# A two-block fp32 transformer layer: a weight piece and the inputs taken in halves, one mLSTM head scored earlier, two steps moved to POOL and ACT

## What is computed

```python
k, v = split(rmsnorm(mem, g_mem) @ w_mem_kv)             # memory keys and values
q_a, k_a, ... = split(rmsnorm(x, g_mix) @ w_in)
u = rms_norm(x, norm_g) @ w_in                            # mLSTM and pool layer
xm, om, gates, zm, xp, zp = split(u)
xc = silu(causal_conv(xm, conv_w, conv_b))                # width 4
q, k = xc_h @ w_q, xc_h @ w_k * 256 ** -0.5               # per head of 256
v = xm_h @ w_v
hm = mlstm(q, k, v, gates) * sigmoid(om)
hm = rms_norm per head, + skip * xc, * silu(zm)
out = concat(hm, pool(xp) ...) @ w_out + x
```

## Time and profile before

| | |
|---|---|
| median of 3 runs | 819.34 us (818.83 to 819.68) |
| the profiled execution | 819.23 us |
| its span | 817.4 us |
| PE, DVE, ACT, POOL busy | 794.1, 568.0, 432.3, 131.0 us |
| mean granted clock of TensorE | 0.992 |
| DMA | 142.78 MB, 175 GB/s in the mean |

### The profile page before, as it was taken

The page is one execution under the profiler, slowest core; times in us unless marked ns, Lnnn a source line. Parts: engine busy times, 40 slices in busy tenths (PEclk is TensorE's granted clock), DMA queues, the critical chain, the costliest instruction groups (busy, mean ns, idle before and its releaser), DMA issues.

```text
span 817.4 us, 11950 instructions
## 1 busy us (share of the span) xinstructions
PE 794.1 (97%) x4616; PEld 693.7 (85%) x4616; DVE 568.0 (69%) x946; ACT 432.3 (53%) x585; POOL 131.0 (16%) x99
## 2 busy tenths in 40 slices
PE   8799999999999999999999999999999979999998
PEld 7688788888888899999988888989799868877776
DVE  5645556796468678787864485769865795997774
ACT  5834544344544466566553374555736343788450
POOL 0002740000000004544431000041005000024000
PEclk9899999999999999999999999999999999999999
DMA  9977433334455465554555545435565414634211
GB/s 342 360 278 247 155 139 123 145 109 163 152 202 192 168 245 210 165 197 176 186 172 191 203 148 170 170 134 155 191 214 200 154 52 155 251 127 154 87 52 52
DMA packets 23364, 142.78 MB, mean 175 GB/s; under 512 B 3564, under 2 KB 4472, under 8 KB 7312
## 3 DMA queue, kind: packets, MB, share of 16 engines
q1 hardware_dynamic: 20160, 134.51, 46.0%
q0 software_dynamic: 1376, 3.43, 1.4%
q10 hardware_dynamic: 1776, 4.12, 1.4%
HBM read 140.97 MB, written 2.64 MB: 176 GB/s over the span
## 4 chain that ended last, share of the span: by engine, by line
PE 78%; DVE 13%; ACT 4%; issue 2%; DMA 2%; SPq 0%; ACTq 0%; DVEq 0%
PE gemm L488 16%; PE gemm L490 15%; PE gemm L489 15%; PE gemm L494 8%; PE gemm L495 8%; PE gemm L496 8%; DVE wlo L1662 4%; ACT whi L1161 2%; DMA raw<-in_weights 2%; DVE xc L2183 2%; PE head L554 1%; PE head L885 1%; PE head L744 1%; PE head L884 1%; PE head L905 1%
## 5 line engine op out<-in xcount | busy, mean ns | idle before, releaser
L1662 DVE TENSOR_TENSOR wlo<-raw,whi 128x2048 fp32r<-128x2048 f32 x122 | 282.1, 2314 | 115.9 <-ACT whi L1161 115.7
L1161 ACT CAST whi<-raw 128x2048 fp32r<-128x2048 f32 x122 | 232.6, 1906 | 210.1 <-PE gemm L490 124.3
L488 PE MATMUL gemm<-whi,x0hi 128*128 128x512 f32 (+2 forms) x400 | 158.0, 395 | 5.7 <-DVE x0lo L1849 4.2
L490 PE MATMUL gemm<-whi,x0lo 128*128 128x512 f32 (+2 forms) x400 | 154.6, 386 | 0.0
L489 PE MATMUL gemm<-wlo,x0hi 128*128 128x512 f32 (+2 forms) x400 | 154.3, 386 | 0.0
L494 PE MATMUL gemm<-x1hi,whi 128*128 128x256 f32 x400 | 113.5, 284 | 0.0
L495 PE MATMUL gemm<-x1lo,whi 128*128 128x256 f32 x400 | 113.2, 283 | 0.0
L496 PE MATMUL gemm<-x1hi,wlo 128*128 128x256 f32 x400 | 113.2, 283 | 0.0
L488 PEld LDWEIGHTS gemm<-whi,x0hi 128*128 128x128 f32 x400 | 75.7, 189 | 22.1 <-DVE x0lo L1849 4.9
L490 PEld LDWEIGHTS gemm<-whi,x0lo 128*128 128x128 f32 x400 | 75.5, 189 | 15.0
L489 PEld LDWEIGHTS gemm<-wlo,x0hi 128*128 128x128 f32 x400 | 75.8, 190 | 13.5
(11 more groups left out here) (344 smaller groups left out, 1346.6 us busy)
## 6 DMA issues: line engine op xcount, KB each, us to landing
raw<-in_weights SPq DMA_DIRECT2D x122, 1024.0 KB, 4.8
raw<-in_weights SPq DMA_DIRECT2D x4, 512.0 KB, 6.3
bias_rows<-bias_row POOLq DMA_DIRECT2D x1, 1536.0 KB, 15.6
memt<-in_memt SPq DMA_DIRECT2D x4, 256.0 KB, 5.3
tok<-in_mem SPq DMA_DIRECT2D x1, 1024.0 KB, 7.7
xt<-in_xt SPq DMA_DIRECT2D x2, 512.0 KB, 11.1
xres<-in_x ACTq DMA_DIRECT2D x1, 1024.0 KB, 6.5
bias<-bias_rows POOLq DMA_DIRECT2D x8, 128.0 KB, 2.9
```

What stands on the lines that cost most here:

```text
L488: mm(o, xh, wh, start=start, stop=False)
L490: return mm(o, xl, wh, start=False, stop=stop)
L1161: nc.scalar.copy(whi[:, p % RING, :], raw[:, p % RING, :]).then_inc(s_hi, 1)
L1662: V.tensor_tensor(wlo[:, p % RING, :], raw[:, p % RING, :], whi[:, p % RING, :].bitcast(F32), ALU.subtract).then_inc(s_lo, 1)
```

## The change

- Piece 2 is split in halves and multiplied by `first_pieces`, at its own bank. The load of the larger part of the parameters goes behind that of the memory, and the half scalings that need it to step 4.
- The squares of the memory are summed in step 0. The input pairs are scaled two in step 1 and two in step 2, and PE waits for two pairs before piece 4 and for all before piece 5.
- The first two xm pieces wait for chunk c - 4.
- `x1hi` and `x1lo` of xc are taken without the factor 0.5, which goes into the emptying of wq and wk; the low parts are taken by POOL.
- `ML0` is 98. Head 0 is scored in wk after its third chunk, and everything of the heads comes one step earlier.
- `rsqrt` has two steps of a higher order, nine operations in all instead of eleven.
- DVE multiplies the root by half and by the reciprocal, and ACT scales the head by it.

```diff
-ML0 = p0("aout")
+ML0 = p0("aout") - 1
-SCALED = {"mem": 1, "mix": 3, "ckv": p0("cu") + 3, "cq": p0("ukv")}
+SCALED = {"mem": 0, "mix": 3, "ckv": p0("cu") + 3, "cq": p0("ukv")}
...
             half_piece(1, 1)
-            sp.dma_start(par[:, GAINS:NPAR], ins["params"][:, GAINS:NPAR]).then_inc(s_par, 16)
...
             sp.dma_start(tok[:, 12:14, :, :].rearrange("p a b c -> p (a b c)"), ins["mem"]).then_inc(s_mem, 16)
+            sp.dma_start(par[:, GAINS:NPAR], ins["params"][:, GAINS:NPAR]).then_inc(s_par, 16)
             next_piece(3)
...
                 e = p - ML0
-                if not 0 <= e <= ML_H + 1:
+                if not 1 <= e <= ML_H + 1:
                     return
-                if e == 0:
-                    pe.wait_ge(s_vones, 1)
-                    pe.wait_ge(s_gcol, 1)
-                    pe.wait_ge(s_mixlo, 4)
...
-                for p in range(2):
+                for p in range(3):
+                    o = [bank(p // 2, t) for t in range(T)]
                     for half in range(2):
-                        pair = 2 * p + half
+                        pair = (2 * p + half) % 4
...
-            for p in range(2, Z0):
+            for p in range(3, Z0):
...
-                if p == p0("qkv"):
-                    pe.wait_ge(s_inlo, 8)
+                if p in (p0("qkv"), p0("qkv") + 1):
+                    pe.wait_ge(s_inlo, 6 + 2 * (p - p0("qkv")))
...
-                    chunk_free(pe, c - 2)
+                    chunk_free(pe, c - (4 if name == "xm" and i_ < 2 else 2))
...
+                        if name == "wk" and g == 2:
+                            pe.wait_ge(s_vones, 1)
+                            pe.wait_ge(s_gcol, 1)
+                            ml_score(0).then_inc(s_mo, 1)
...
+                if 1 <= e <= ML_H:
+                    h = e - 1
+                    act.wait_ge(s_mr, h + 1)
+                    for t in range(T):
+                        i = nc.scalar.activation(hm[h % 2][:, t, :], hm[h % 2][:, t, :], ACT.Copy,
+                                                 scale=rstd[:, 16 + 2 * h + t:17 + 2 * h + t])
+                    i.then_inc(s_mn, 1)
...
-                    nc.scalar.activation(x1hi[:, 2 * i:2 * i + 2, :], xc[:, 2 * i:2 * i + 2, :],
-                                         ACT.Copy, scale=0.5).then_inc(s_fhi, 1)
+                    nc.scalar.copy(x1hi[:, 2 * i:2 * i + 2, :], xc[:, 2 * i:2 * i + 2, :]).then_inc(s_fhi, 1)
...
-                                                    ACT.Copy, scale=1.0 if name == "wq" else 1.0 / 16)
+                                                    ACT.Copy, scale=0.5 if name == "wq" else 0.5 / 16)
...
+            split_half(2, 0)
+            split_half(2, 1)
             for p in range(Z0):
-                if p not in LATE_SPLIT:
+                if p not in LATE_SPLIT and p > 0:
                     split(p + 2)
...
-                if p == 2:
-                    input_hi("mix", range(4))
+                if p in (1, 2):
+                    input_hi("mix", (2 * p - 2, 2 * p - 1))
...
-                for n in range(3):
-                    order(V.tensor_tensor(u, dst, dst, ALU.mult))
-                    order(V.tensor_tensor(u, u, v, ALU.mult))
-                    last = V.scalar_tensor_tensor(dst, u, 1.5, dst, ALU.add, ALU.mult)
-                    if n < 2:
-                        order(last)
-                return last
+                order(V.tensor_tensor(u, dst, dst, ALU.mult))
+                order(V.tensor_tensor(u, u, v, ALU.mult))
+                order(V.scalar_tensor_tensor(u, u, 5.0 / 3, u, ALU.add, ALU.mult))
+                order(V.scalar_tensor_tensor(dst, u, 1.25, dst, ALU.add, ALU.mult))
+                order(V.tensor_tensor(u, dst, dst, ALU.mult))
+                order(V.scalar_tensor_tensor(u, u, 3.375, v, ALU.mult, ALU.mult))
+                return V.scalar_tensor_tensor(dst, u, 2.25, dst, ALU.add, ALU.mult)
...
-                    order(V.tensor_tensor(r, r, rsum[:, :], ALU.mult))
-                    for t in range(T):
-                        i = V.tensor_scalar(hm[h % 2][:, t, :], hm[h % 2][:, t, :],
-                                            rstd[:, 16 + 2 * h + t:17 + 2 * h + t], 0.5, ALU.mult, ALU.mult)
-                    i.then_inc(s_mn, 1)
+                    V.scalar_tensor_tensor(r, r, 0.5, rsum[:, :], ALU.mult, ALU.mult).then_inc(s_mr, 1)
...
-                i = p - p0("xm") - 3
-                if 0 <= i < 4:
-                    k = slice(2 * i, 2 * i + 2)
-                    dve.wait_ge(s_fhi, i + 1)
-                    V.scalar_tensor_tensor(x1lo[:, k, :], xc[:, k, :], 0.5, x1hi[:, k, :].bitcast(F32),
-                                           ALU.mult, ALU.subtract).then_inc(s_xclo, 1)
...
+            for g in range(4):
+                pool.wait_ge(s_fhi, g + 1)
+                k = slice(2 * g, 2 * g + 2)
+                Q.tensor_tensor(x1lo[:, k, :], xc[:, k, :], x1hi[:, k, :].bitcast(F32),
+                                ALU.subtract).then_inc(s_xclo, 1)
```

More of the change, by code:

```diff
@@ L324, in program @@
         s_vones = sem("value_ones_ready")
+        s_mr = sem("ml_root_ready")
         s_md = sem("max_rows_moved")
@@ L815, in ml_step @@
                 e = p - ML0
-                if not 0 <= e <= ML_H + 1:
+                if not 1 <= e <= ML_H + 1:
                     return
-                if e == 0:
-                    pe.wait_ge(s_vones, 1)
-                    pe.wait_ge(s_gcol, 1)
-                    pe.wait_ge(s_mixlo, 4)
[L822 to L826, removed]
+                pe.wait_ge(s_mp, min(e, ML_H))
+                if e >= 2:
+                    pe.wait_ge(s_mden, e - 1)
                 if 1 <= e <= ML_H:
@@ L986, in first_pieces @@
             def first_pieces():
-                for p in range(2):
+                for p in range(3):
+                    o = [bank(p // 2, t) for t in range(T)]
                     for half in range(2):
-                        pair = 2 * p + half
+                        pair = (2 * p + half) % 4
                         pe.wait_ge(s_hi if half else s_hi0, p + 1)
                         pe.wait_ge(s_inhi, pair + 1)
[L993 to L996, removed]
+                        order_ = [(t, 2 * pair + j, slice((2 * half + j) * 512, (2 * half + j) * 512 + 512))
+                                  for t in range(T) for j in range(2)]
+                        for t, kb, ws in order_:
+                            mm(o[t][:, :], x1hi[:, kb, t * P:t * P + P], whi[:, p, ws], start=kb == 0, stop=False)
                         pe.wait_ge(s_lo if half else s_lo0, p + 1)
-                        for t, j in order_:
-                            kb, ws, ts = 4 * p + j, slice(j * 512, j * 512 + 512), slice(t * P, t * P + P)
-                            mm(bank(0, t)[:, :], x1hi[:, kb, ts], wlo[:, p, ws], start=False, stop=False)
+                        for t, kb, ws in order_:
+                            mm(o[t][:, :], x1hi[:, kb, t * P:t * P + P], wlo[:, p, ws], start=False, stop=False)
                         pe.wait_ge(s_inlo, pair + 1)
-                        for t, j in order_:
-                            kb, ws, ts = 4 * p + j, slice(j * 512, j * 512 + 512), slice(t * P, t * P + P)
-                            i = mm(bank(0, t)[:, :], x1lo[:, kb, ts], whi[:, p, ws], start=False,
+                        for t, kb, ws in order_:
+                            i = mm(o[t][:, :], x1lo[:, kb, t * P:t * P + P], whi[:, p, ws], start=False,
                                    stop=kb == KB - 1)
@@ L1269, in split_half @@
             def split_half(p, h):
-                act.wait_ge(s_piece[p] if h else s_half_piece[p], 16)
+                act.wait_ge(s_piece[p] if h or p == 2 else s_half_piece[p], 16)
                 nc.scalar.copy(whi[:, p, h * D:h * D + D], raw[:, p, h * D:h * D + D])\
@@ L2239, in _ @@
             split_half(1, 1)
-            dve.wait_ge(s_par, 16)
-            for o, (name, w) in ((0, ("gn", 4)), (4, ("pool_scale", 8)), (12, ("skip", 8))):
-                a = PCOL[name][0]
-                i = V.tensor_scalar(half[:, o:o + w], par[:, a:a + w], 0.5, None, ALU.mult)
-            order(i)
+            split_half(2, 0)
+            split_half(2, 1)
             for p in range(Z0):
@@ L2261, in _ @@
                 gates_dve(p)
-                if p == 2:
-                    input_lo("mix", range(4))
+                if p == 4:
+                    dve.wait_ge(s_par, 16)
+                    for o, (name, w) in ((0, ("gn", 4)), (4, ("pool_scale", 8)), (12, ("skip", 8))):
+                        a = PCOL[name][0]
+                        i = V.tensor_scalar(half[:, o:o + w], par[:, a:a + w], 0.5, None, ALU.mult)
+                    order(i)
+                if p in (1, 2):
+                    input_lo("mix", (2 * p - 2, 2 * p - 1))
                 if p == 20:
```

## The result

The changed kernel took 806.33 us in the median of 4 runs (806.18 to 806.52), the kernel before 819.12 in the same session: a ratio of 0.9843 (95% interval 0.9826 to 0.9860), 12.8 us less. The profiled execution took 806.28 us, with a span of 804.5.

A forecast was written before the change was run, and what follows sets the result against it. PE, busy 97% of the 817.4 us span, was taken as the bound. Gains 6.4 + 1.7 + 3.6 = 11.7, less 1.7 for one new half-speed stretch, net 10.0: 819.2 - 10.0 = 809.2 us, range 803.5 to 814.0.

The forecast's parts named there:

- The start: Before piece 4: PE's 4.15 us wait for the input's low parts and 2.25 of half clock go, 6.4 us saved.
- Piece 2's halves: At the start: splitting piece 2 in halves gains nothing, since PE then idles 1.4 us for piece 3 instead.
- The pool chunk: Before the first xm pieces: PE released 1.6 us earlier and no half clock behind it, 1.7 more, 3.3 us together.
- The lock between DVE and POOL: In xm and om: POOL's low-part operations block DVE for their whole length, 2 x (1.47 - 0.69) = 1.6 us lost.
- The mLSTM heads: Heads one piece earlier: 3.6 us saved, with a loop of 9.3 to 9.4 us a head and some waits left.
- The new half-speed stretch: Behind one of the new idle stretches of 1.9, 1.4 and 2.1 us the clock falls once, 1.7 us lost.
- Elsewhere PE has no gap worth taking: Outside the start, the pool chunk and the mLSTM heads, PE has no idle time worth saving; no gain counted.
- the slower one: Rival, mLSTM heads: ACT's hold delays weight casts, 12.5 us a turn, 822.0 us; decides from 11.8; chance 0.05.
- The lock did not fall the other way: Rival, xm and om: DVE goes first each time and POOL waits, stage worth 4.7 us, 806.2 us; chance 0.09.
- The input halves don't help: Rival, start: later loads make PE wait 3 to 4 us at piece 4 or 6, 813.1 to 815 us; chance 0.10.

The follow-up runs named there:

- the run with all casts first: The changed kernel with ACT's scaling of every mLSTM head moved behind the next weight cast instead of ahead of it: 809.2 us.

## Why the prediction was right

Forecast 809.2, measured 806.33; the range held it. Step by step:

- **The start**, 6.4 forecast, 6.06 measured. The place of the gain was right, and so were the wait that stays at 24 to 25 and the half clock, and PE waits for none of the pieces behind. The credit was not: the text gives the pairs' early place as much part as the squares and does not name the root behind the squares, which held ACT for 2.37 us. By the experiments the squares are worth 4.8, and the remaining 1.2 go to PE's shorter wait or to the early pairs, of which one would have done. The sum came out right without telling these apart.
- **Piece 2's halves**, nothing forecast, nothing measured; the halves were not even what moved the wait.
- **The pool chunk**, 3.3 forecast, 3.07 measured. By the traces 1.57 of it are the wait (2.02 to 0.45) and 1.5 the clock. Undone alone, the wait cost 1.3 at the end of the kernel, and the clock 2.0 in two of four executions and nothing in the others.
- **The lock between DVE and POOL**, two times 1.47 - 0.69 = 1.6 forecast, 1.00 lost in the trace and 1.0 given back by the experiment. The mechanism stands, POOL waiting when DVE turns to the silu; an operation costs DVE 1.10, not 1.47, since POOL, once DVE's subtraction was over, took 1.15 and not 1.47. By the Trainium skill (SBUF — State Buffer, section "SBUF: two separate sides"), an operation that holds the shared port pair keeps it for its whole length and the other blocks; the trace agrees, since DVE's silu lasts 1.78 us and ends when POOL's 2.10 us operation has ended and 0.55 have passed.
- **The mLSTM heads**, 3.6 forecast, 4.07 measured. The loop of 9.3 to 9.4 us a head is 9.27 (636.06 to 645.33). Forecast waits 1.0, 2.1 and 0.5; measured 0.71, 1.86 and 0.55. Undone alone, the earlier start of the heads costs 3.5 and the old root 2.6 (0.7 of it in the attention heads), while ACT's scaling has lost 1.45 against DVE's.
- **The new half-speed stretch**, 1.7 us against the change: this term was wrong. None appeared: the four runs have mean clocks of 0.999 and 1.000 and lie within 0.34 us of each other. The longest wait left, 1.86 (1.85 to 1.88 in the other kernels that have it), did not lower the clock in any profile of these experiments.
- **"Elsewhere PE has no gap worth taking"** was wrong by 0.70 us. The shorter root saves that in the attention heads, where no single wait of PE is above 0.2 us, so that the table of waits does not show it. The old root brings it back.

The forecast's terms as measured give 6.06 + 3.07 - 1.00 + 4.07 = 12.2, and with 0.70 the 12.9 of the spans. Of the 2.9 us by which the forecast was high, 1.7 are the stretch that did not come, 0.7 the root, and the rest the sizes. Of the rivals, the slower one asked for 11.8 us a turn, and the longest in the changed kernel took 9.27. The lock did not fall the other way: POOL went first at all three silus beside it. That this rival's 806.2 is next to the measured time is chance. "The input halves don't help" asked for a wait of 3 to 4 us at piece 4 or 6 because of later loads, and none came; that the early pairs add nothing beside PE's shorter wait has another reason.

## What to carry to other kernels

When a change has several parts at one place, undo each alone: here one number in a table of steps (the squares, moved into a wait for a load) was worth most of the start, while the halves of piece 2, with far more code, were worth nothing. Undoing one part shows what it is worth beside the others: where two parts take away the same wait, each looks worthless alone. Before work goes to an idle engine that shares a port with the busy one, set its price there against what it blocks: 0.69 us saved cost 1.10. Of the two steps that this change moved to POOL and ACT, neither paid: back on DVE they gave 0.96 and 1.45 us. And when an in-order engine must hold for a result, compare for every turn what stands behind it with what that itself waits for; the better order differed between the first head and the last.

## What the runs showed of the hardware

The granted clock's fall from its higher level (2.4 GHz) to half of it behind a wait is not fixed by the length of the wait. The program that waits 2.01 us for a pool chunk ran two executions at a mean clock of 1.000 (807.6) and two at 0.998 (809.7), 2.0 us longer. In the profiles the clock fell after waits of 2.02 (twice), 2.17, 2.18, 2.25, 2.28, 2.45 and 4.15 us, not after others of 2.01 and 2.24, nor after 1.86, and not even after the 3.05 us of the run with all casts first (its stretch of 658 to 668):

```profile
658.00:668.00 10.00, 7.73 (x36) 6.52 (x37) 5.81 (x8) 6.38 (x9) 1.65 (x4) 1.00 0.51 166
```

So a wait of 2 to 3 us has to be priced as itself and a chance of about 2 us more. Kernels with several such waits scattered more: the one with only the squares moved spread over 3.4 us and the kernel before over 3.7 in the same session (though over 0.9 in the first), the changed one over 0.3. That the waits are the cause of the scatter is likely by the mean clocks, but not shown by a trace of each execution.

DVE's and POOL's operations on two inputs in SBUF did not run side by side here. POOL's subtraction ended 1.15 us after DVE's, and DVE's silu 0.55 us after POOL's, and the time that each stood is in its own record (2.10 us on POOL, 1.78 instead of 0.68 on DVE).
